# Gated linear attention on one core: decay exponents from products with 0/1 matrices, heads written out, gates inside the projections

## What is computed

```
def _gla_chunked(q, k, v, log_a):        # one direction; the other gets flipped inputs
    bc = jnp.cumsum(to_chunks(log_a), axis=3)
    def step(state, inp):
        q_c, k_c, v_c, b_c = inp
        dec = jnp.exp(jnp.where(causal, b_c[:, :, :, None, :] - b_c[:, :, None, :, :], -jnp.inf))
        scores = jnp.einsum('bhid,bhjd,bhijd->bhij', q_c, k_c, dec)
        ...
def _mixer_gla(h, w_in, gate_w2, gate_b, norm_g, w_out):
    proj = jnp.matmul(h, w_in)                       # q, k, v, r and a rank-16 gate input per direction
    gate_logit = jnp.einsum('bsnr,nrk->nbsk', gl, gate_w2) + gate_b
    log_a = jax.nn.log_sigmoid(gate_logit) / 16.0    # one log decay per token and key channel
    ...
    o = _rmsnorm(o_f + o_b, norm_g) * jax.nn.silu(r) # per head
    return jnp.matmul(o, w_out)
```

## Time and profile before

| | us |
|---|---|
| median of 3 runs | 1673.27 (1670.94 to 1675.42) |
| profiled execution, its own time | 1678.58 |
| span of its profile | 1676.9 |
| PE busy | 1452.7 (87%) |
| DVE busy | 987.7 (59%) |
| ACT busy | 764.4 (46%) |
| POOL busy | 385.8 (23%) |

### The profile page before, as it was taken

How to read it: one execution, slowest core, us unless ns; L and a number is a source line. 1 busy time by engine, 2 the same in 40 slices (tenths; PEclk the granted TensorE clock), 3 DMA queues, 4 the chain that set the end, 5 groups by cost and what they waited for, 6 DMA issues and landing times.

```text
span 1676.9 us, 27900 instructions
## 1 busy us (share of the span) xinstructions
PE 1452.7 (87%) x10864; PEld 1391.7 (83%) x10864; DVE 987.7 (59%) x1632; ACT 764.4 (46%) x1156; POOL 385.8 (23%) x359
## 2 busy tenths in 40 slices
PE   2789999988988999989998899999896455799997
PEld 2779999988888999989887789999795344799997
DVE  4577877657656554499455557744534443576542
ACT  2324555564343333555834446633443332366433
POOL 1116764305200000366333020000200553020000
PEclk9789999999999999999999999999998555899998
DMA  8656543234636745544200046655353000355540
GB/s 285 218 176 219 179 149 110 93 101 166 215 115 223 229 141 170 150 141 138 75 1 1 1 126 182 194 177 176 103 176 101 0 0 0 101 151 185 180 162 26
DMA packets 202483, 223.57 MB, mean 133 GB/s; under 512 B 7617, under 2 KB 197740, under 8 KB 200332
## 3 DMA queue, kind: packets, MB, share of 16 engines
q1 hardware_dynamic: 197232, 220.21, 41.1%
q10 hardware_dynamic: 5147, 1.92, 0.5%
HBM read 221.07 MB, written 1.05 MB: 132 GB/s over the span
## 4 chain that ended last, share of the span: by engine, by line
PE 71%; DVE 12%; ACT 6%; POOL 4%; issue 3%; DMA 2%; ACTq 1%; DVEq 0%; POOLq 0%; SPq 0%
PE acc L548 17%; PE acc L550 16%; PE acc L549 16%; DVE GB L1463 2%; PE acc L486 2%; PE acc L487 2%; PE acc L493 2%; PE pm L605 1%; ACT whi L421 1%; POOL DD L917 1%; DVE ADA L1332 1%; DMA raw<-in_w_ffn_in 1%; DVE spt L1392 1%; PE acc L2315 1%; PE pm L600 1%
## 5 line engine op out<-in xcount | busy, mean ns | idle before, releaser
L548 PE MATMUL acc<-HH,whi 128*128 128x256 f32 x1728 | 501.0, 290 | 30.4 <-ACT whi L421 9.4
L421 ACT ACTIVATE whi<-raw 128x1024 fp32r<-128x1024 f32 (+2 forms) x380 | 379.3, 1030 | 305.4 <-PE acc L550 200.2
L549 PE MATMUL acc<-HL,whi 128*128 128x256 f32 x1728 | 496.0, 287 | 0.0
L550 PE MATMUL acc<-HH,wlo 128*128 128x256 f32 x1728 | 495.7, 287 | 0.0
L431 DVE TENSOR_TENSOR wlo<-raw,whi 128x1024 fp32r<-128x1024 f32 (+2 forms) x292 | 337.1, 1186 | 212.9 <-ACT whi L421 210.6
L548 PEld LDWEIGHTS acc<-HH,whi 128*128 128x128 f32 x1728 | 339.0, 196 | 36.6 <-issue 18.0
L549 PEld LDWEIGHTS acc<-HL,whi 128*128 128x128 f32 x1728 | 339.2, 196 | 0.3 <-issue 0.2
L550 PEld LDWEIGHTS acc<-HH,wlo 128*128 128x128 f32 x1728 | 338.9, 196 | 0.0
L431 POOL TENSOR_TENSOR wlo<-raw,whi 128x1024 fp32r<-128x1024 f32 x88 | 214.0, 2451 | 461.5 <-ACT whi L421 458.4
L548 PE MATMUL acc<-HIDH,whi 128*128 128x256 f32 x688 | 195.7, 284 | 6.4 <-ACT whi L421 4.5
L550 PE MATMUL acc<-HIDH,wlo 128*128 128x256 f32 x688 | 195.4, 284 | 0.0
(11 more groups left out here) (467 smaller groups left out, 2403.5 us busy)
## 6 DMA issues: line engine op xcount, KB each, us to landing
raw<-in_mlp_w SPq DMA_DIRECT2D x64, 1024.0 KB, 5.7
raw<-in_w_in SPq DMA_DIRECT2D x36, 1024.0 KB, 5.4
raw<-in_w_ffn_in SPq DMA_DIRECT2D x22, 1024.0 KB, 5.5
raw<-in_a_w_in SPq DMA_DIRECT2D x16, 1024.0 KB, 5.5
raw<-in_w_ada_mix SPq DMA_DIRECT2D x12, 1024.0 KB, 6.8
raw<-in_w_ada_ffn SPq DMA_DIRECT2D x12, 1024.0 KB, 5.5
raw<-in_b_w_in SPq DMA_DIRECT2D x12, 1024.0 KB, 5.3
raw<-in_w_ssm_out SPq DMA_DIRECT2D x8, 1024.0 KB, 5.2
```

The lines of the kernel that those rows point to most:

```text
L421: act.activation(whi[:, (s.t0 + 2 * u + h) % 4, 0:k], raw[:, place(s, b, u) % 4, 0:k, h * P:h * P + P], ACT.Copy).then_inc(hi_ready, 1)
L548: pe.matmul(acc[:, q, 0:T], whi[:, slot, i], hh, start=first and i == 0, stop=False)
L549: pe.matmul(acc[:, q, 0:T], whi[:, slot, i], hl, start=False, stop=False)
L550: m = pe.matmul(acc[:, q, 0:T], wlo[:, slot, i], hh, start=False, stop=final and i == k - 1)
```

## The change

The prefix sums, POOL's differences and the per-head copies go. The log decays are kept token-major (tokens on the partitions), in two fp32r parts `LAH` and `LAL`. The exponents of a level are their product with a 0/1 matrix that says which tokens are summed for each output token; PE makes two levels at a time, both directions (`exponents`, 8 matmuls of 256 columns), and ACT takes Exp straight from the accumulator (`GE`). POOL builds the 0/1 matrices `W05` and `W67` with memsets and affine selects while the MLP of the layer before runs. The four heads are written out as 16 steps g of two levels each. Exponents run two steps ahead, `KQ` has four buffers, the scores two, `SS` two; K and Q are read from `QK2` and the values from `VT2` without copies, and at level 0 K isn't multiplied. The values product of head h-1 stands in the first step of head h (`values`), its sums of squares in the third (`value_sums`); ACT copies and squares the result. Normalising and splitting are done in two halves (heads 0, 1 and 2, 3), the gating before the normalising.

The gates move into the projections: PE's product with `ws3` after block 0 of b_qk, that with `gw` (with the bias as a 33rd row) after block 2, and the log sigmoid in four parts of 128x512 on ACT (`log_gate`, `gate_hi`) and DVE (`gate_log`, `gate_lo`) at the ends of the blocks of b_qk, b_v and b_r. `gw` is cleared by POOL right after the layer norm ln1_0, long before ACT issues its DMAs (four instead of two).

```diff
+        GE = [ar(f"GE{u}", 40 + 4 * u, [P, 2, 2, T]) for u in range(2)]
+        W67 = ar("W67", 64, [P, 2, 2, 2 * P], F32R)
+        W05 = ar("W05", 84, [P, 3, 2, 2 * P], F32R)
...
+            c.link(pool.memset(gw[:], 0.0))
+            c.link(pool.memset(glt[NH:NH + 1, :], 1.0))
+            pool.nop().then_inc(gz, 1)
+            def keep(v, cm, base_, pattern):
+                c.link(pool.affine_select(out=v, in_=v.bitcast(F32), compare_op=ALU.is_ge, fill=0.0, base=base_,
+                                          pattern=pattern, channel_multiplier=cm))
+            def sums_to(dst, lv, d):
+                b = 1 << lv
+                n_ = P // (2 * b)
+                c.link(pool.memset(dst.bitcast(F32), 1.0))
+                left, right = (dst.rearrange("p (n t b) -> p n t b", t=2, b=b)[:, :, side] for side in range(2))
+                keep(left, 1, -1 if d == 0 else 0, [[-2 * b, n_], [-1, b]])
+                keep(left, -1, b - 1, [[2 * b, n_], [0, b]])
+                keep(right, -1, b if d == 0 else b - 1, [[2 * b, n_], [1, b]])
+                keep(right, 1, -b, [[-2 * b, n_], [0, b]])
+            for lv in range(6):
+                for d in range(2):
+                    sums_to(W05[:, lv // 2, d, lv % 2 * P:lv % 2 * P + P], lv, d)
+            pool.wait_ge(hid_lo, 32 + 4)
+            for tk, sides in enumerate(((slo[:, 0:P], maskb[:, P:2 * P]), (maskf[:, 0:P], suo[:, 0:P]))):
+                for d in range(2):
+                    sums_to(W67[:, tk, d, 0:P], 6, d)
+                    c.link(pool.tensor_copy(W67[:, tk, d, P:], sides[d]))
+            pool.nop().then_inc(w_ok, 1)
...
+            def log_gate(q):
+                act.wait_ge(lg_p, q + 1)
+                act.activation(LT[:, q], pm[:, q], ACT.Abs).then_inc(lt_e, 1)
+                act.wait_ge(lt_e, 3 * q + 1)
+                act.activation(LT[:, q], LT[:, q], ACT.Exp, scale=-1.0).then_inc(lt_e, 1)
+                act.wait_ge(lt_e, 3 * q + 2)
+                act.activation(LT[:, q], LT[:, q], ACT.Ln, bias=1.0).then_inc(lt_e, 1)
+            def gate_hi(q):
+                act.wait_ge(la_ok, q + 1)
+                act.activation(LAH[:, q], LA[:, q], ACT.Copy).then_inc(lh_ok, 1)
+            def qk_more(b):
+                if b == 1:
+                    act.wait_ge(gl_p, 1)
+                    act.activation(glt[0:NH], pm[0:NH, 3, 0:T], ACT.Copy).then_inc(gl_ok, 1)
+                elif b == 3:
+                    act.preload_act_table_set("natural_log_exp_and_others")
+                    log_gate(0)
+            def v_more(b):
+                if b:
+                    gate_hi(b - 1)
+                if b < 3:
+                    log_gate(b + 1)
+                else:
+                    gate_hi(3)
...
+            def head_copy(h):
                 act.wait_ge(bo_p, h + 1)
+                o_ = pm[:, 2].rearrange("p (e t) -> p e t", e=2)
+                act.activation(H[:, 2 * h:2 * h + 2], o_, ACT.Copy).then_inc(hc_ok, 1)
+                act.activation(SQX[:, 2 * h:2 * h + 2], o_, ACT.Square).then_inc(bo_ok, 1)
+            def head_std(i):
+                act.wait_ge(l2_sum, 2 * i + 2)
+                inv_sqrt(act, RS[:, 2 * i:2 * i + 2], pm[:, 3].rearrange("p (e t) -> p e t", e=2), T, 0, l2_std)
+            def heads_hi(i):
+                act.wait_ge(hr2_ok, i + 1)
+                act.activation(HH[:, 4 * i:4 * i + 4], H[:, 4 * i:4 * i + 4], ACT.Copy).then_inc(n_hh, 4)
+            act.preload_act_table_set("natural_log_exp_and_others")
+            for g in range(4 * B_HEADS):
+                h, p = divmod(g, 4)
+                for tk in range(NT):
+                    act.wait_ge(gx_p, 2 * g + tk + 1)
+                    if g > 1:
+                        act.wait_ge(kq_ok, 2 * g - 2)
+                    act.activation(GE[g % 2][:, :, :, tk * P:tk * P + P].rearrange("p l d c -> p d l c"),
+                                   acc[:, 2 * (g % 2) + tk].rearrange("p (d l c) -> p d l c", d=2, l=2), ACT.Exp,
+                                   scale=1.0 / 16).then_inc(gx_ok, 1)
+                if h and p == 1:
+                    head_copy(h - 1)
+                elif h == 2 and p == 3:
+                    head_std(0)
+                elif h == 3 and p == 2:
+                    heads_hi(0)
+            head_copy(3)
+            head_std(1)
+            heads_hi(1)
...
+            def gate_log(q):
+                v.wait_ge(lt_e, 3 * q + 3)
+                v.scalar_tensor_tensor(LA[:, q], pm[:, q], 0.0, LT[:, q], ALU.min, ALU.subtract).then_inc(la_ok, 1)
+            def gate_lo(q):
+                v.wait_ge(lh_ok, q + 1)
+                v.tensor_tensor(LAL[:, q], LA[:, q], LAH[:, q].bitcast(F32), ALU.subtract).then_inc(ll_ok, 1)
+            def v_more(b):
+                gate_log(b)
+                if b > 1:
+                    gate_lo(b - 2)
+            def r_more(b):
+                if b < 2:
+                    gate_lo(b + 2)
+            split_section(v, split_lo, SEC["b_qk"], None)
+            split_section(v, split_lo, SEC["b_v"], None, extra=v_more)
+            split_section(v, split_lo, SEC["b_r"], None, extra=r_more)
...
+            def decayed(g, i):
+                h, lv = g // 4, g % 4 * 2 + i
+                n, b = 2 * g + i, 1 << lv
+                if n >= 4:
+                    v.wait_ge(sc_p, 9 * ((n - 4) // 8) + (n - 4) % 8 + 2)
+                v.wait_ge(gx_ok, 2 * g + 2)
+                e_ = GE[g % 2][:, i]
+                def with_side(d, step):
+                    s_ = e_[:, d]
+                    return bass.AP(tensor=s_.tensor, offset=s_.offset, ap=[s_.ap[0], [2 * b, P // b], [step + b, 2], [1, b]])
+                def sides(ap):
+                    return ap.rearrange("p (n t b) -> p n t b", t=2, b=b)
+                if lv:
+                    v.tensor_tensor(sides(KQ[:, n % 4, 0]), with_side(0, T), sides(QK2[:, 4 + h]), ALU.mult)
+                v.tensor_tensor(sides(KQ[:, n % 4, 1]), with_side(1, -T), sides(QK2[:, h]), ALU.mult).then_inc(kq_ok, 1)
...
+            def take(g, i):
+                h, lv = g // 4, g % 4 * 2 + i
+                s_ = 9 * h + lv + 1
+                ss = SS[h % 2]
...
+                if lv == 0:
+                    v.wait_ge(sc_p, s_)
+                    if h > 1:
+                        v.wait_ge(bo_p, h - 1)
+                    v.scalar_tensor_tensor(half_of(ss[:, 0, 0:P]), found(s_ - 1), 2.0, id2, ALU.mult, ALU.mult)\
+                     .then_inc(s_ok, 1)
+                v.wait_ge(sc_p, s_ + 1)
...
+                    v.copy_predicated(half_of(ss[:, 0, 0:P]), mask.bitcast(I32), found(s_)).then_inc(s_ok, 1)
+                else:
+                    cross = ss[:, 0, P:T]
+                    cross = bass.AP(tensor=cross.tensor, offset=cross.offset, ap=[cross.ap[0], [P, 2], [1, P]])
+                    v.tensor_copy(cross, found(s_)).then_inc(s_ok, 1)
...
+            for g in range(4 * B_HEADS):
+                h, p = divmod(g, 4)
+                for i in range(2):
+                    decayed(g, i)
+                    if g:
+                        take(g - 1, i)
+                if h and p == 2:
+                    gated(h - 1)
+                if h == 3 and p == 1:
+                    normed(0)
+                elif h == 3 and p == 3:
+                    heads_lo(0)
+            for i in range(2):
+                take(15, i)
+            gated(3)
+            normed(1)
+            heads_lo(1)
...
+            def gate_logits(b):
+                if b == 0:
+                    pe.wait_ge(full_ok, 8 * FULL["ln2_0"] + 8)
+                    for k in range(DT):
+                        m = pe.matmul(pm[0:NH, 3, 0:T], ws3[:, k], X[:, k], start=k == 0, stop=k == DT - 1)
+                    m.then_inc(gl_p, 1)
+                elif b == 2:
+                    pe.wait_ge(gl_ok, 1)
+                    pe.wait_ge(gw_in, 16 * 4)
+                    for tk in range(NT):
+                        for d in range(2):
+                            pe.matmul(pm[:, 2 * tk + d], glt[:, tk * P:tk * P + P], gw[:, d], start=True, stop=True)\
+                              .then_inc(lg_p, 1)
+            pe_section(pe, SEC["b_qk"], hrhs, ready=h_parts("ln2_0"), after=gate_logits)
             pe_section(pe, SEC["b_v"], hrhs, tok_major=True)
             pe_section(pe, SEC["b_r"], hrhs)
+            def exponents(g):
+                h, p = divmod(g, 4)
+                for tk in range(NT):
+                    if g > 1:
+                        pe.wait_ge(gx_ok, 2 * g - 4 + tk + 1)
+                    for d in range(2):
+                        o_ = acc[:, 2 * (g % 2) + tk, d * T:d * T + T]
+                        w_ = W05[:, p, d] if p < 3 else W67[:, tk, d]
+                        pe.matmul(o_, LAH[:, 2 * tk + d, h * P:h * P + P], w_, start=True, stop=False)
+                        m = pe.matmul(o_, LAL[:, 2 * tk + d, h * P:h * P + P], w_, start=False, stop=True)
+                    m.then_inc(gx_p, 1)
```

(41 more changed lines are left out.)

206 lines of the change are left out of this document (38 added, 168 removed).

## The result

The changed kernel takes 1592.3 us (median of 4 runs, 1588.26 to 1594.02), where the kernel before took 1674.35 in the same set (4 runs, 1670.94 to 1675.82): ratio 0.9509, 95% interval 0.9484 to 0.9534, 82.1 us less. The forecast was 1587, the range 1574 to 1618.

What follows compares the result with a forecast made beforehand. The bound was taken as a chain of latencies after the GLA projections, partly PE at half clock. The stage: 73.0 + 3.0 + 56 + 8.3 + 6.3 = 146.6 us for 232.6; 1673.3 - 86 = 1587, range 1574 to 1618.

Steps and rivals of the forecast that it cites:

- the likeliest case: Whole kernel: the forecast of 1587 us itself, own range 1580 to 1598, chance 0.52.
- The gw product is 3.5 us, all on the path: Projections, b_qk: the product with gw, 8 passes of 512 columns, adds 3.5 us to the path.
- So this first product is free: After block 0 of b_qk: PE's product with ws3, 3.59 us before, fits in the hole and costs nothing.
- PE no longer enters block 1 at half clock: Block 1 of b_qk: some 16 matmuls no longer run slow, 1.5 us gained, between 0 and 1.5.
- I take 0.5 us of stalls in all: Projections: gate work on ACT delays weight splits by only 0.5 us in all; bounds 0 and 14.
- B: Projections: ACT's gate work starves them, evacuations in b_v 6.5 us or more apart; +13.5 us, 1600; chance 0.1.
- DVE is the bound by work: Head loop: DVE has the most work, 8.2 to 10.3 us a head plus 0.9 gating; busy over 8 of 10.
- That is some 1.5 us a head: Start of each head: late diagonal and values ahead of scores on PE delay DVE by some 1.5 us.
- I add 3 for stretches in which the clock falls: Head loop: 3 us added to 53 for stretches of lower clock, giving 56.
- Rival A: Head loop: the clock stays at half, loop 88 us and end +3, 1622 us; chance 0.2.
- Rival C: Head loop: runs at DVE's pace with the values hidden, 45 us, time 1576; chance 0.15.
- Rival D: Head loop: hops don't overlap, 8.4 us a step, slower than before at 1699 us; chance 0.02.

Runs made afterwards that it cites:

- the run with the gates outside: Changed kernel with gate products, log sigmoid and splitting moved back behind the last projection: 1593.18 us, ratio 0.9528.
- the run with ACT's order changed: Changed kernel with ACT's log sigmoid of a block ahead of the evacuation in b_v, not behind it: 1589.86 us, ratio 0.950.
- the combined version: Changed kernel with ACT's head copy later, log sigmoid before evacuation in b_v and b_qk, diagonal earlier, X product one block later: 1575.48 us, ratio 0.9424.

## Why the forecast held, and where not

**The result** is 5.3 us above 1587, inside the likeliest case's own range. The stage is 3.7 longer than forecast; before's median in this set is 1.1 higher than the one the forecast started from; the rest is below the scatter of the medians. That the total came so near is in part luck, since the loop, its largest term, came out right by errors that cancel (below). "A stage outside 1206 to 1439 that moves by more than 3 us" was a sign of being wrong, and the part ahead differs by 8.3 in the two profiled executions; but that is the scatter of single executions, as said above, and the medians differ by the stage alone.

**"The gw product is 3.5 us, all on the path": right** (3.70 with its tail, 1214.46 to 1218.09). **"So this first product is free": mostly.** X comes from POOL, whose 8 operations took 10.28 us, while before they took 8.38:

```profile
1188.86 10.28 POOL L674 TENSOR_SCALAR X<-SQX,par 128x256 f32<-128x256 f32 x8 [90.36 <-DVE SQX L652]
```

and the forecast had looked at ACT and DVE as what this hole waits for, not at POOL, which cost 1.2 us. Seven of the eight took the same time in both kernels; the last, beside DVE's split of the next weights, took 2.8 us and not 0.9. **"PE no longer enters block 1 at half clock": right there**, at 1202.76 it goes on at 0.12; but the half clock came back 16 us later, behind the second product, for 1.5 us, so that the term stands at 0 and not at -1.5. The clearing alone gave 5.3 in the run with the gates outside, where the forecast had 3.6 and 1.5.

**"I take 0.5 us of stalls in all": mis-sized, 2.3.** (6.85 - 5.75) + (6.94 - 5.75), both beyond the 6.5 that the forecast gave as the sign of B, though B's size isn't reached. The step that failed is "its first half done 1.22 later at 1238.4, and PE wants it when block 1 ends: 2.8 us of cover". In b_v (`tok_major`) PE multiplies with both halves of a block's weights from the first matmul on, and waits for both. The whole split of the earlier trace rows ends at 1237.21 + 2.36 = 1239.57, which leaves 1.7 us to 1241.23 and not 2.8. The rows of the changed kernel at the last block of b_v show it:

```profile
1243.03 2.36 DVE L430 TENSOR_TENSOR wlo<-raw,whi 128x1024 fp32r<-128x1024 f32 x2 [4.40 <-ACT whi L420]
...
1245.65 0.36 PE L539 MATMUL acc<-whi,HH 128*128 128x256 f32 x1 [0.96 <-DVE wlo L430]
```

PE goes on 0.26 us after the second half. ACT's added work there is 2.35 us (1239.51 to 1241.86), so the cover of 1.66, less that step of 0.26, falls 0.95 short, and PE's wait is 0.96. The other stall, 0.87 at 1232.95, again ends 0.25 after DVE's second half (1232.70), though the profile names ACT's evacuation beside it; in the run with ACT's order changed PE goes on at this border 0.25 after DVE's half (1237.76) while the evacuation has only begun (1237.67). Ahead of that split stand the table load and the log sigmoid at the end of b_qk. Rival B with its 13.5 was this mechanism at six times its size. The three terms, 1.2 + 1.5 + 1.8, are 4.5 of the 4.7 by which this part exceeded the forecast, and the combined version, which has none of them, takes 72.69 for the 73.0 forecast.

**The start of the loop, the end: right** (2.81 for 3.0, 8.23 for 8.3). b_out's block 0 took 5.10 for 6.3: no slow start. In six of the eight variants of the changed kernel it is 6.5 to 6.6, near the forecast, in two 5.1; what decides between the two was not looked for.

**The loop: right in size (56.41 for 56) by luck, wrong in its account.** Three parts of it don't stand. "DVE is the bound by work": it is busy 36.9 of 55 us, not over 8 of 10, and it gets there only in the combined version (38.1 of 45.2). The forecast's lower end of 45 for "DVE at 0.34 throughout, 11 a head" doesn't follow from its own terms either: 24 operations at 0.34 and the gatings are 9.1 a head, and 11.2 is what the spacing of 0.43 gives. "That is some 1.5 us a head" for PE's order with diagonal and values: the break costs 4 us and more and is ACT's, which the forecast listed as work (6.3 us a head) and never as a queue; moved, it gave 8.2. "I add 3 for stretches in which the clock falls": it fell only from 1320 on, to 0.83 and then 0.66; its price wasn't measured by itself. What was left out at the breaks is about what the steps within a head were counted too slow. From one diagonal to the next it took 10.3, 14.3 and 15.7 us, not 12 to 14 throughout; the first head, with no break ahead of it, is the pace of the loop.

**Rival A (half clock in the loop): refuted.** 1.00 for 40 us, with PE busy 6.4 to 8.9 of 10 and waiting several times a step. The Trainium skill (TensorE: Matmul & The Clock Gate, A second HAM failure mode: psum-queue depth-cycling) tells of a kernel in which short idles between groups of matmuls make the clock swing between its levels. The trace doesn't bear that out here but for the last head (0.83 and 0.66). **Rival C (45 us, the values hidden)** has the length that the combined version reached, 45.23, but not its reason: PE was the busier engine (40.1 us to DVE's 38.1), and 45 wasn't DVE's closest pace. **Rival D** (its own terms add up to 184 us, not 179) is far off; even without overlap across heads the loop is 67.

**POOL's matrices** were ready long before they were wanted: their last piece ends at 1098.5, the norm begins at 1188.86.

```profile
1086.67 2.85 POOL L896 TENSOR_SCALAR_AFFINE_SELECT W<-W 128x64 fp32r<-128x64 f32 x4
...
1098.20 0.29 POOL L916 CAST W<-suo 128x128 fp32r<-128x128 f32 x1
```

**Where the gain comes from**, as far as runs separate it: in the loop, three quarters of POOL's differences carry 22 to 30 us and the clock about 7 (parts of these two are the same time, so they don't add to more than 30), and the order across heads holds 11 of what was won, some 8 as order and the rest mainly through the clock. Dropping the prefix sums and passing the gates on in parts gives 10; moving the gates into the projections is worth 3.6 more by the stage, and nothing that the time can show. The end (28.61 to 8.23: half of the norm under the last head's steps, statistics straight from the values) has no run of its own, nor has the removal of the copies at a head's start; 20 us of the gain are thus read from the trace and not isolated.

## What to carry to other kernels

When work of one unit is laid over the next, write down the order of every engine's queue, not only of the two that do the work: an engine that is 40% busy and waits for one late result holds up everything queued behind it, and moving its copy down by a step was worth 8 us here. A cover ends where the last of the operands that the consumer waits for must be ready, not the first: b_v wanted both halves of a split, and a cover of 2.8 us was one of 1.7. When a run is taken as the price of one thing, look at the clock in it too: of 11 us and of 30 us here, some 3 and up to 7 were clock. And a stage's length may come out right by two errors, so the forecast's account has to be tested at its parts, by busy shares and by the spacing of steps.

## What was not expected of the hardware

- Adding 8 products of 256 columns to each of 32 levels made the old kernel 9.7 us faster (ratio 0.9936 [0.9921, 0.9951]), with the granted clock of its loop at 0.81 and not 0.54.
- The clock fell to half about 4 us after the start of a product of 33 rows by 512 columns (3.70 us long) in all seven kernels that had waited 1.2 us for X some 15 us earlier, with PE busy throughout from that wait on, and not in the one in which that wait was gone.
- In a loop with PE busy 6.4 to 8.9 of 10 and waits of about 1 us in each step the clock stayed at its upper level for 40 us; it fell in the window behind the one with 6.4. Without the overlap across heads it fell to 0.50 for 12 us, and DVE waited 10.83 us at that break, 6.05 at the others.
- POOL's 8 operations on X took 10.28 us in the nine new kernels and 8.38 in the three old ones, on the same work. The difference is in the last operation, 2.8 us for 0.9: in the new kernels a DVE split of 2.35 us (1196.08 in the changed kernel) ran beside it, in the old none did. That this is the cause wasn't isolated.
